# Further expert passes joined to the main pass: their gate and up matmuls, their row fetches and their scatters in a two-layer MoE kernel

## The chip, the cores and the metric

The kernel runs on one core of a Trainium2 chip. The metric is the device time of one execution in microseconds, as the median over several runs. The profile is one execution, recorded by the hardware profiler.

## The reference, cut to what matters

One inference step of a small diffusion backbone: 128 prompt tokens and 256 latent tokens, width 1024, two layers. Layer 0 mixes tokens by differential attention, layer 1 by a Fourier transform. Behind each mixer stands a mixture of experts: a router picks one of 4 groups and in it 2 of 8 experts, so that each of the 384 tokens goes to 2 of 32 gated MLPs.

```python
a = jnp.einsum('nd,edf->nef', t, w_g)          # gate, 1024 -> 256
u = jnp.einsum('nd,edf->nef', t, w_u)          # up,   1024 -> 256
act = jax.nn.silu(a) * u * combine[..., None]  # zero except for the 2 experts of a token
y = jnp.einsum('nef,efd->nd', act, w_d)        # down, 256 -> 1024
x = _post_norm(x, g_f * moe, ln_gain[i, 1], ln_bias[i, 1])
```

## The kernel before

The kernel computes an expert only for its own tokens, in float32. Experts are handled in 16 pairs per layer (`PAIRS`); one **pass** of a pair takes up to 64 tokens (`CAP`) for each of its two experts, which makes 128 rows. Where an expert of the pair has more than 64 tokens, the pair needs **further passes**, up to 5. VectorE counts the tokens (`route`), and packs the number of further passes of each pair, three bits each, into two words (`mem.words`, one for pairs 0 to 7 and one for 8 to 15). Every engine loads these words into a register and loops over the pairs with the loops and branches of `passes` (line 307; POOL and SP have their own loops). `b` is the parity of the pair; most buffers come in two, by parity.

A main pass of pair n, by engine:

- **POOL** (GpSimd) fetches the rows of pair n + 2 from `h_scratch` in HBM into `G[b]` with an indirect gather (`gather`, DMA issue on line 563, behind a copy of the indices on line 559), and writes the pair's results to `y_scratch` with an indirect scatter from `O[b]` (`scatter`, line 576, index copy line 570). A counter `o_free` tells ScalarE and VectorE when `O[b]` may be written.
- **PE** multiplies gate and up (`gate_up`, line 916) into bank b, turns the rows of pair n + 1 (`gt`, line 903), turns the activations (`act_transposes`, line 924) and multiplies down (`down`, line 938) into banks 5 and 6. In the profile's names all on-chip buffers of this stage are `arena`.
- **ScalarE** takes the SiLU of the gate (line 1215), evicts half of the turned rows (line 1210) and half of the result (`o_evict`, line 1220). **VectorE** multiplies by up (`up_times`, line 1662), evicts the other halves (lines 1657 and 1672) and the turned activations (line 1666).
- **SP** loads weights. The ring has four slots, one per expert, two pairs in all. Gate and up of pair n + 2 are issued when pair n, further passes included, has used its own (`u_ps` and `gate_up_through`), down when all its downs are done (`d_ps` and `down_through`, which VectorE raises behind the further pass's `o_evict`). SP waits for these in program order.

A further pass stood behind the whole main pass, as the body of `passes`. On POOL its rows were fetched into `G[2]` in the same pair's turn, and the queue waited for the landing of the main scatter before the further pass could write `O[b]`, and for the landing of its own scatter before going on:

```python
pool.wait_ge(S["gt_ps"], n1)
with pool.If(times > 0):
    gather(extra, l, PAIRS + n, pool.snap(further[pool]), 2)
gather(S, l, n + 2, n + 2, b)
pool.wait_ge(S["scattered"], n16)
scatter(S, l, n, n, b)
with pool.If(times > 0):
    pool.wait_ge(S["scattered"], n32)
    scatter(extra, l, (r + 1) * PAIRS + n, k, b)
    pool.wait_ge(extra["scattered"], k16)
```

## Time and profile before

| | before |
|---|---|
| median of 3 runs | 1063.76 us (1063.31 to 1065.43) |
| the profiled execution | 1065.38 us, span 1063.6 us |
| PE busy | 835.2 us (79%) |
| VectorE, ScalarE, POOL busy | 329.9, 166.0, 158.7 us |
| DMA moved | 318.11 MB, mean 299 GB/s |
| chain that ended last | PE 50%, DMA 35% |

The span runs from the first to the last instruction. Busy time is the time in which an engine executed something; the chain of waits follows the last instruction back through what released each step. All times in the rows below are microseconds from the start of the span.

### The profile page before, as it was taken

Reading aid. Unit: us, or ns where it says so; the run is one execution under the profiler, and the core shown is the slowest. Engines: PE = TensorE matmul, PEld = TensorE weight load, DVE = VectorE, ACT = ScalarE, POOL = GpSimd, SP = SyncE. Lnnn points to the kernel's source line nnn. Section 1 sums busy time; section 2 is a strip of 40 time slices with the busy share of each in tenths; the row PEclk is TensorE's granted clock in tenths of the full one; section 3 lists DMA queues with packets and bytes.
Section 4 is the critical chain, followed back from the end, with each engine's and each line's share of the span. In section 5 each row is a group of like instructions: output and inputs, shape, how many; then the busy total and the mean of one; then the engine's idle time right before and its main releaser. Section 6 shows DMA issues by size and latency. Waiting matters only on the chain.

```text
span 1063.6 us, 13809 instructions
## 1 busy us (share of the span) xinstructions
PE 835.2 (79%) x4921; PEld 442.9 (42%) x4922; DVE 329.9 (31%) x803; ACT 166.0 (16%) x354; POOL 158.7 (15%) x245
## 2 busy tenths in 40 slices
PE   3899999969987888988778855997589877787740
PEld 3556565635466333323323334664533322332310
DVE  2113555544754111111111128247411110111117
ACT  0122222233010111111111112110111111101110
POOL 1032030311111120211101101101111111101010
PEclk9999999989985999989989987999589998999985
DMA  9992653292686496999999889564659999999831
GB/s 336 367 350 91 220 176 130 80 367 82 235 328 248 165 417 260 420 421 420 419 412 407 347 309 375 204 252 178 227 217 421 420 420 419 419 417 413 368 127 79
DMA packets 90242, 318.11 MB, mean 299 GB/s; under 512 B 13150, under 2 KB 26174, under 8 KB 65624
## 3 DMA queue, kind: packets, MB, share of 16 engines
q1 hardware_dynamic: 70016, 274.60, 65.3%
q0 software_dynamic: 13376, 22.16, 6.0%
q10 hardware_dynamic: 6808, 20.79, 5.1%
q8 instruction: 27, 0.44, 0.2%
q14 instruction: 15, 0.12, 0.0%
HBM read 315.82 MB, written 26.80 MB: 322 GB/s over the span
## 4 chain that ended last, share of the span: by engine, by line
PE 50%; DMA 35%; DVE 6%; issue 4%; SPq 2%; ACT 2%; POOL 1%; ACTq 0%; DVEq 0%; POOLq 0%
DMA ring<-in_w_expert_up 24%; PE psum L916 15%; PE psum L799 8%; DMA ring<-in_w_ada 6%; PE psum L745 6%; PE psum L938 4%; PE psum L694 4%; PE psum L771 3%; DMA arena<-h_scratch,gidx 2%; DMA y_scratch<-arena,sidx 2%; PE psum L903 1%; DMA arena<-y_scratch 1%; SPq L366 1%; PE psum L1091 1%; PE psum L850 1%
## 5 line engine op out<-in xcount | busy, mean ns | idle before, releaser
L916 PE MATMUL psum<-ring,arena 128*64 128x512 f32 x1088 | 260.0, 633 | 60.6 <-DMA ring<-in_w_expert_up 56.6
L916 PEld LDWEIGHTS psum<-ring,arena 128*64 128x64 f32 x1088 | 93.4, 146 | 223.2 <-issue 221.1
L938 PE MATMUL psum<-ring,arena 128*64 128x512 f32 x544 | 125.9, 604 | 30.9 <-DVE arena L1666 29.6
L1662 DVE TENSOR_TENSOR arena<-arena,psum 128x256 f32<-128x256 f32 x34 | 14.3, 421 | 309.6 <-ACT arena L1215 309.6
L799 PE MATMUL psum<-ring,hT 128*128 128x384 f32 x288 | 98.2, 495 | 0.0
L938 PEld LDWEIGHTS psum<-ring,arena 128*64 128x64 f32 x544 | 40.2, 138 | 93.2 <-issue 77.8
L694 PE MATMUL psum<-ring,silu 128*32 128x128 f32 x1536 | 55.8, 305 | 27.4 <-DMA ring<-in_w_ada 26.9
L576 POOL DMA_INDIRECT y_scratch<-arena,sidx x34 | 34.4, 1012 | 250.9 <-DVE arena L1672 250.9
L745 PE MATMUL psum<-ring,hT 128*128 128x512 f32 x160 | 70.2, 595 | 1.1 <-ACT hT L1288 0.7
L799 PEld LDWEIGHTS psum<-ring,hT 128*128 128x128 f32 x288 | 54.5, 194 | 35.0 <-issue 1.5
L1672 DVE COPY arena<-psum 128x512 f32<-128x512 f32 x34 | 23.5, 692 | 134.4 <-PE psum L938 134.4
L694 PEld LDWEIGHTS psum<-ring,silu 128*32 128x32 f32 x1536 | 47.6, 123 | 38.1 <-DMA ring<-in_w_ada 19.1
L1215 ACT ACTIVATE arena<-psum 128x256 f32<-128x256 f32 x34 | 13.0, 383 | 273.6 <-PE psum L916 273.6
L903 PEld LDWEIGHTS psum<-k_rows_sb,arena 128*128 128x128 f32 x288 | 35.5, 195 | 33.6 <-issue 26.0
L903 PE MATMUL psum<-k_rows_sb,arena 128*128 128x128 f32 x288 | 42.6, 292 | 5.3 <-DMA arena<-h_scratch,gidx 5.3
L745 PEld LDWEIGHTS psum<-ring,hT 128*128 128x128 f32 x160 | 30.1, 191 | 38.1 <-issue 36.3
L563 POOL DMA_INDIRECT arena<-h_scratch,gidx x38 | 39.7, 1044 | 30.8 <-POOL gidx L559 29.2
L1220 ACT COPY arena<-psum 128x512 f32<-128x512 f32 x34 | 19.9, 585 | 151.3 <-PE psum L938 151.3
L504 POOL TENSOR_TENSOR rstd<-rs_v,power 128x1 f32<-128x1 f32 (+2 forms) x19 | 11.3, 593 | 173.6 <-DVE rs_v L1347 173.6
L771 PE MATMUL psum<-ring,hT 128*128 128x384 f32 x96 | 33.3, 508 | 3.7 <-ACT hT L1150 2.3
L1196 ACT ACTIVATE arena<-psum,nb 128x384 f32<-128x384 f32 (+1 forms) x48 | 24.0, 505 | 49.7 <-DVE nb L1437 49.7
L828 PE MATMUL psum<-arena 64*128 64x384 f32 (+1 forms) x96 | 19.3, 476 | 14.7 <-ACT arena L1196 9.7
(177 smaller groups left out, 796.6 us busy)
## 6 DMA issues: line engine op xcount, KB each, us to landing
ring<-in_w_expert_gate SPq DMA_DIRECT2D x64, 1024.0 KB, 14.1
ring<-in_w_expert_up SPq DMA_DIRECT2D x64, 1024.0 KB, 21.4
ring<-in_w_expert_down SPq DMA_DIRECT2D x64, 1024.0 KB, 19.3
ring<-in_w_ada SPq DMA_DIRECT2D x24, 2048.0 KB, 14.0
ring<-in_w_qkv SPq DMA_DIRECT2D x9, 1024.0 KB, 11.5
arena<-m_scratch POOLq DMA_DIRECT2D x12, 512.0 KB, 7.4
h_scratch<-h ACTq DMA_DIRECT2D x6, 1024.0 KB, 10.3
arena<-y_scratch ACTq DMA_DIRECT2D x6, 1024.0 KB, 7.7
```

Source lines behind the costliest of these rows:

```text
L563: pool.indirect_dma_start(mem.G[b], None, h_dram[l], bass.IndirectOffsetOnAxis(ap=mem.gidx[:, b:b + 1].bitcast(U32), axis=0), bounds_check ...
L576: pool.indirect_dma_start(y_dram[l], bass.IndirectOffsetOnAxis(ap=mem.sidx[:, b:b + 1].bitcast(U32), axis=0), mem.O[b], None, bounds_check ...
L694: last = pe.matmul(out[32 * j:32 * j + 32, :], mem.silu[:, k, :], w[:, k, P * j:P * j + P], start=(k == 0), stop=(k == KC - 1))
L745: last = pe.matmul(bank[banks[half]], mem.hT[:, k, P * t:P * t + P], w[:, k, :], start=(k == 0), stop=(k == KC - 1))
L771: last = pe.matmul(bank[FIRST_BANKS[g]][:, 0:384], mem.hT[:, k, P * t:P * t + P], w[:, k, 384 * half:384 * half + 384], start=(k == 0), st ...
L799: last = pe.matmul(bank[i % 2][:, 0:384], mem.hT[:, k, P * t:P * t + P], w[:, k, 384 * half:384 * half + 384], start=(k == 0), stop=(k == ...
L903: last = pe.transpose(bank[2 + c // 4][:, P * (c % 4):P * (c % 4) + P], mem.G[b][:, c::KC], ident)
L916: last = pe.matmul(bank[b][64 * e:64 * e + 64, :].rearrange("p (g n) -> p g n", g=2), mem.GT[b][:, c, 64 * e:64 * e + 64], w, start=(c == ...
L938: last = pe.matmul(bank[5 + half][64 * e:64 * e + 64, :], mem.actT[b][:, f, 64 * e:64 * e + 64], w[:, f, 512 * half:512 * half + 512], sta ...
L1196: nc.scalar.activation(mem.p[g % 2][j][:, 0:w], bank[5 + j][:, 0:w], ACT.Exp, bias=mem.nb[:, g % 2, j:j + 1], scale=SCALE, accum_out=mem.s ...
L1220: nc.scalar.copy(mem.O[b][:, 0:512], bank[5]).then_inc(S["o_act"], 1)
L1672: V.tensor_copy(mem.O[b][:, 512:D], bank[6]).then_inc(S["o_dve"], 1)
```

## The change

The numbers of further passes are packed into four words: the two as before, and two shifted by one pair, so that a place in them tells of the pair that follows.

On PE, ScalarE and VectorE `passes` now has four parts: `begin` (gate and up of the main pass), then either `alone` (the rest of a main pass without further ones) or `joined`: the further rows are turned, the main activations are turned, gate and up of the first further pass are multiplied, and only then come the main pass's down and the turning of the next pair's rows. `more` finishes a further pass, and starts it too where it is the second or later.

On POOL the rows of a pair's first further pass are fetched in the turn of the pair before, and those of pair 0 ahead of the loop. The scatter of a further pass has a third index column, and its landing is awaited in the next pair's turn (`past`), ahead of the signal `o_free`. The wait for the main scatter stands between that scatter and the further one, as before.

```diff
-        self.words_f = sb("words_f", [P, 2])
-        self.words = sb("words", [P, 2], I32)
+        self.words_f = sb("words_f", [P, 4])
+        self.words = sb("words", [P, 4], I32)
...
-        self.sidx = sb("sidx", [P, 2], I32)
+        self.sidx = sb("sidx", [P, 3], I32)
...
+        self.octals = small(2, PAIRS)
...
-        def passes(eng, l, S, first, body):
...
+        def passes(eng, l, S, begin, alone, joined, more):
...
-                        first(n, b, half * (PAIRS // 4) + it)
                         times = eng.snap((word >> (it * 6 + 3 * b)) & 7, min_val=0, max_val=PASSES - 1)
+                        begin(n, b, half * (PAIRS // 4) + it)
                         with eng.If(times > 0):
+                            joined(n, b, half * (PAIRS // 4) + it, eng.snap(further[eng]))
                             with eng.Fori(0, times) as r:
-                                body(n, b, r + 1, eng.snap(further[eng]))
+                                more(n, b, r, eng.snap(further[eng]))
                                 eng.reg_add(further[eng], further[eng], 1)
+                        with eng.Else():
+                            alone(n, b, half * (PAIRS // 4) + it)
...
+                if l == 0:
+                    pool.dma_start(mem.landing[2:3, :], A["k_rows"][0:1, 0:P]).then_inc(extra["scattered"], 16)
 
                 pool.wait_ge(words_done, l + 1)
+                begin = pool.value_load(mem.words[0:1, 0:1], min_val=0, max_val=(1 << 24) - 1)
+                with pool.If(pool.snap(begin & 7) > 0):
+                    gather(extra, l, PAIRS, pool.snap(further[pool]), 2)
                 with pool.Fori(0, 2) as half:
                     word = pool.value_load(mem.words[0:1, bass.ds(half, 1)], min_val=0, max_val=(1 << 24) - 1)
+                    coming = pool.value_load(mem.words[0:1, bass.ds(half + 2, 1)], min_val=0, max_val=(1 << 24) - 1)
                     with pool.Fori(0, PAIRS // 4) as it:
                         for b in range(2):
                             n = half * (PAIRS // 2) + it * 2 + b
                             n1, n16, n32 = value(n + 1), value(16 * n + 16), value(16 * n + 32)
+                            past = value(16 * pool.snap(further[pool]) + 16)
                             pool.wait_ge(S["gt_ps"], n1)
-                            pool.sem_inc(turns, 1)
-                            times = pool.snap((word >> (it * 6 + 3 * b)) & 7, min_val=0, max_val=PASSES - 1)
-                            with pool.If(times > 0):
-                                gather(extra, l, PAIRS + n, pool.snap(further[pool]), 2)
                             gather(S, l, n + 2, n + 2, b)
                             pool.wait_ge(S["scattered"], n16)
+                            pool.wait_ge(extra["scattered"], past)
                             pool.sem_inc(S["o_free"], 1)
-                            scatter(S, l, n, n, b)
+                            times = pool.snap((word >> (it * 6 + 3 * b)) & 7, min_val=0, max_val=PASSES - 1)
+                            following = pool.snap((coming >> (it * 6 + 3 * b)) & 7, min_val=0, max_val=PASSES - 1)
                             with pool.If(times > 0):
-                                pool.wait_ge(S["scattered"], n32)
-                                pool.sem_inc(turns, 1)
+                                scatter(S, l, n, n, b, b)
                                 with pool.Fori(0, times) as r:
                                     k = pool.snap(further[pool])
                                     k16 = pool.snap(16 * k + 16)
                                     with pool.If(r > 0):
                                         gather(extra, l, (r + 1) * PAIRS + n, k, 2)
+                                    pool.wait_ge(S["scattered"], n32)
+                                    pool.wait_ge(extra["scattered"], k16)
                                     pool.sem_inc(extra["o_free"], 1)
-                                    scatter(extra, l, (r + 1) * PAIRS + n, k, b)
-                                    pool.wait_ge(extra["scattered"], k16)
-                                    pool.sem_inc(turns, 1)
+                                    scatter(extra, l, (r + 1) * PAIRS + n, k, b, 2)
                                     pool.reg_add(further[pool], further[pool], 1)
+                                with pool.If(following > 0):
+                                    gather(extra, l, PAIRS + 1 + n, pool.snap(further[pool]), 2)
+                            with pool.Else():
+                                with pool.If(following > 0):
+                                    gather(extra, l, PAIRS + 1 + n, pool.snap(further[pool]), 2)
+                                scatter(S, l, n, n, b, b)
                 pool.wait_ge(S["scattered"], 16 * PAIRS + 16)
+                pool.wait_ge(extra["scattered"], value(16 * pool.snap(further[pool]) + 16))
...
-                def first(n, b, it):
-
+                def begin(n, b, it):
                     slots = [2 * b + e for e in range(2)]
                     gate_up(S, n, b, slots, [(landed[i], 32 * (it + 1 + l * EXPERTS // SLOTS)) for i in slots])
+
+                def own_down(n, b, it):
+                    slots = [2 * b + e for e in range(2)]
+                    down(S, n, b, slots, [(down_landed[i], 16 * (it + 1 + l * EXPERTS // SLOTS)) for i in slots])
+
+                def alone(n, b, it):
                     gt(S, n + 1, 16 * it + (16, 32)[b], 1 - b)
                     act_transposes(S, n, b)
-                    down(S, n, b, slots, [(down_landed[i], 16 * (it + 1 + l * EXPERTS // SLOTS)) for i in slots])
-
-                def body(n, b, r, k):
+                    own_down(n, b, it)
+
+                def joined(n, b, it, k):
+                    gt(extra, k, 16 * k + 16, 2)
+                    act_transposes(S, n, b)
+                    gate_up(extra, k, b, [2 * b + e for e in range(2)], [])
+                    own_down(n, b, it)
+                    pe.wait_ge(extra["gt_act"], k + 1)
+                    pe.wait_ge(extra["gt_dve"], k + 1)
+                    gt(S, n + 1, 16 * it + (16, 32)[b], 1 - b)
+
+                def more(n, b, r, k):
                     slots = [2 * b + e for e in range(2)]
-                    pe.wait_ge(S["gt_act"], n + 2)
-                    pe.wait_ge(S["gt_dve"], n + 2)
-                    gt(extra, k, 16 * k + 16, 2)
-                    gate_up(extra, k, b, slots, [])
+                    with pe.If(r > 0):
+                        pe.wait_ge(S["gt_act"], n + 2)
+                        pe.wait_ge(S["gt_dve"], n + 2)
+                        gt(extra, k, 16 * k + 16, 2)
+                        gate_up(extra, k, b, slots, [])
                     act_transposes(extra, k, b)
                     pe.wait_ge(S["o_act"], n + 2)
                     pe.wait_ge(S["o_dve"], n + 2)
                     down(extra, k, b, slots, [])
...
-                link(V.tensor_tensor(mem.further, mem.further, mem.const("octal"), ALU.mult))
+                link(V.tensor_tensor(mem.octals[:, 0, :], mem.further, mem.const("octal"), ALU.mult))
+                link(V.tensor_tensor(mem.octals[:, 1, 0:PAIRS - 1], mem.further[:, 1:], mem.const("octal")[:, 0:PAIRS - 1],
+                                     ALU.mult))
+                link(V.memset(mem.octals[:, 1, PAIRS - 1:], 0.0))
                 dve.wait_ge(table_ps, 2 * l + 2)
                 table_evict(slice(PAIRS, PASSES * PAIRS), bank[1][:, 0:(PASSES - 1) * PAIRS])
-                link(V.tensor_reduce(mem.words_f[:, :], mem.further.rearrange("p (h n) -> p h n", h=2), AX, ALU.add))
+                link(V.tensor_reduce(mem.words_f[:, :], mem.octals.rearrange("p w (h n) -> p (w h) n", h=2), AX, ALU.add))
...
-                def first(n, b, it):
-
+                def begin(n, b, it):
                     up_times(S, n, b)
+
+                def alone(n, b, it):
                     gt_evict(S, n + 1, 1 - b)
                     at_evict(S, n, b)
                     o_evict(S, n, b)
 
-                def body(n, b, r, k):
+                def joined(n, b, it, k):
                     gt_evict(extra, k, b)
+                    at_evict(S, n, b)
                     up_times(extra, k, b)
                     dve.sem_inc(gate_up_through, 1)
+                    o_evict(S, n, b)
+                    gt_evict(S, n + 1, 1 - b)
+
+                def more(n, b, r, k):
+                    with dve.If(r > 0):
+                        gt_evict(extra, k, b)
+                        up_times(extra, k, b)
+                        dve.sem_inc(gate_up_through, 1)
                     at_evict(extra, k, b)
                     o_evict(extra, k, b)
                     dve.sem_inc(down_through, 1)
```

ScalarE's parts are cut and ordered like VectorE's; the semaphores of the unused fetch counters are gone.

PE, expert loop of layer 0, pair 0 (L916 gate and up, L903 rows turned, L924 activations turned, L938 down; `main0` and `extra` are the semaphores of main and further passes; rows with a count alone are left out). Before:

```order
L916 MATMUL psum<-ring,arena 64x512 x15
...
L903 MATMUL psum<-k_rows_sb,arena 128x128 [waits gathered1_main0]
...
L924 MATMUL psum<-k_rows_sb,arena 128x128 [waits act_main0]
...
L938 MATMUL psum<-ring,arena 64x512 [waits o_act_main0,o_dve_main0,down_landed1,down_landed0]
...
L319 COMPARE_AND_BRANCH
...
L901 ISA [waits gt_dve_main0,gt_act_main0]
L903 MATMUL psum<-k_rows_sb,arena 128x128 [waits gathered2_extra]
...
L916 MATMUL psum<-ring,arena 64x512 [waits gt_dve_extra,gt_act_extra]
...
L924 MATMUL psum<-k_rows_sb,arena 128x128 [waits act_extra]
...
L938 MATMUL psum<-ring,arena 64x512 [waits o_act_extra,at_sb_extra,o_dve_extra,o_dve_main0,o_act_main0]
```

With the change (L931 gate and up, L918 rows turned, L939 activations turned, L953 down):

```order
L931 MATMUL psum<-ring,arena 64x512 x15
...
L320 COMPARE_AND_BRANCH
...
L918 MATMUL psum<-k_rows_sb,arena 128x128 [waits gathered2_extra]
...
L939 MATMUL psum<-k_rows_sb,arena 128x128 [waits act_main0]
...
L931 MATMUL psum<-ring,arena 64x512 [waits gt_dve_extra,gt_act_extra]
...
L953 MATMUL psum<-ring,arena 64x512 [waits o_act_main0,o_dve_main0,down_landed1,down_landed0]
...
L916 ISA [waits gt_dve_extra,gt_act_extra]
L918 MATMUL psum<-k_rows_sb,arena 128x128 [waits gathered1_main0]
...
L985 COMPARE_AND_BRANCH
...
L939 MATMUL psum<-k_rows_sb,arena 128x128 [waits act_extra]
...
L953 MATMUL psum<-ring,arena 64x512 [waits o_act_extra,at_sb_extra,o_dve_extra,o_dve_main0,o_act_main0]
```

The further gate and up stand ahead of the main down, and their rows are asked for directly behind the main gate and up.

POOL, expert loop of layer 0, even pairs. Before (L563 gather, L576 scatter):

```order
L649 COMPARE_AND_BRANCH
...
L563 DMA arena<-h_scratch,gidx 128x1024 [waits gidx_extra]
...
L563 DMA arena<-h_scratch,gidx 128x1024 [waits gidx_main0]
...
L570 ISA [waits scattered_main0]
...
L576 DMA y_scratch<-arena,sidx 768x1024 [waits o_dve_main0,sidx_main0,o_act_main0]
...
L658 UNCONDITIONAL_BRANCH [waits scattered_main0]
...
L576 DMA y_scratch<-arena,sidx 768x1024 [waits o_act_extra,o_dve_extra]
```

With the change, the even pair's turn with a further pass (L567 gather, L580 scatter), and then the end of the turn: L676 the fetch for the next pair behind a further pass, L679 the same where the pair had none, with the main scatter behind it:

```order
L567 DMA arena<-h_scratch,gidx 128x1024 [waits gidx_main0]
...
L660 ISA [waits scattered_main0]
L664 REGISTER_ALU [waits scattered_extra]
...
L664 COMPARE_AND_BRANCH
...
L580 DMA y_scratch<-arena,sidx 768x1024 [waits o_dve_main0,sidx_main0,o_act_main0]
...
L672 ISA [waits scattered_main0]
L574 ISA [waits scattered_extra]
...
L580 DMA y_scratch<-arena,sidx 768x1024 [waits o_act_extra,o_dve_extra]
```

```order
L676 COMPARE_AND_BRANCH
...
L567 DMA arena<-h_scratch,gidx 128x1024 [waits gidx_extra]
...
L679 COMPARE_AND_BRANCH
...
L567 DMA arena<-h_scratch,gidx 128x1024 [waits gidx_extra]
...
L580 DMA y_scratch<-arena,sidx 768x1024 [waits o_dve_main0,sidx_main0,o_act_main0]
```

The wait for the further scatter moved from behind it into the next turn, where it stands ahead of the fetch for the following pair.

## Rows read from the trace of the kernel before

**Rows 1.** The page's groups: line engine op, out<-in xcount | busy, mean ns | idle

```profile
L1662 DVE TENSOR_TENSOR arena<-arena,psum 128x256 f32<-128x256 f32 x34 | 14.3, 421 | 309.6 <-ACT arena L1215 309.6
```

**Rows 2.** Chain of waits, whole span: start us, us, what

```profile
437.51 20.84 DMA ring<-in_w_expert_up
...
605.40 7.09 PE psum L916 x32
```

**Rows 3.** Stretch of 5 us: engines busy, then PEclk, DMA share, GB/s

```profile
405.00:410.00 5.00, 5.00 (x26) 1.90 (x22) 0.00 (x0) 0.00 (x0) 0.18 (x1) 1.00 0.10 41
```

**Rows 4.** Timeline of PE, 344 to 411: start us, us, operation [idle before]

```profile
344.42 7.09 PE L916 MATMUL psum<-ring,arena 128*64 128x512 f32 x32 [1.09 <-DVE arena L1657]
...
357.60 1.16 PE L903 MATMUL psum<-k_rows_sb,arena 128*128 128x128 f32 x8
359.64 7.09 PE L916 MATMUL psum<-ring,arena 128*64 128x512 f32 x32 [0.88 <-DVE arena L1657]
...
368.86 3.65 PE L938 MATMUL psum<-ring,arena 128*64 128x512 f32 x16 [0.70 <-issue]
372.32 7.07 PE L916 MATMUL psum<-ring,arena 128*64 128x512 f32 x32
...
393.48 1.16 PE L903 MATMUL psum<-k_rows_sb,arena 128*128 128x128 f32 x8 [1.37 <-DMA arena<-h_scratch,gidx]
...
396.05 5.35 PE L938 MATMUL psum<-ring,arena 128*64 128x512 f32 x16 [1.18 <-DVE arena L1666]
...
403.36 7.09 PE L916 MATMUL psum<-ring,arena 128*64 128x512 f32 x32 [0.87 <-DVE arena L1657]
```

**Rows 5.** Timeline of SP's queue: the releases of the weight slots

```profile
367.47 0.35 SPq L366 DMA_DIRECT2D ring<-in_w_expert_gate  x1
...
372.76 1.18 SPq L372 DMA_DIRECT2D ring<-in_w_expert_down  x2
...
411.20 0.34 SPq L366 DMA_DIRECT2D ring<-in_w_expert_gate  x1
...
416.44 0.89 SPq L372 DMA_DIRECT2D ring<-in_w_expert_down  x2
```

**Rows 6.** Source line L563 in 345.8 to 346: the further rows' gather of pair 0

```profile
L563 POOL DMA_INDIRECT arena<-h_scratch,gidx x1: 1079/1079/1079, 345.9 to 345.9; - x1
...
DMA to landing us min/median/max: 7.4/7.4/7.4
```

**Rows 7.** Timeline of POOL, layer 0: gathers L563, scatters L576, index copies

```profile
343.34 0.52 POOL L635 DMA_DIRECT2D landing<-in_k_rows  x1
...
359.34 1.03 POOL L576 DMA_INDIRECT y_scratch<-arena,sidx  x1 [8.25 <-DVE arena L1672]
363.43 0.18 POOL L570 COPY sidx<-table 128x1 int32 x1 [3.06 <-DMA y_scratch<-arena,sidx]
374.07 0.99 POOL L576 DMA_INDIRECT y_scratch<-arena,sidx  x1 [10.45 <-DVE arena L1672]
383.25 0.18 POOL L559 COPY gidx<-table 128x1 int32 x1 [8.19 <-DMA y_scratch<-arena,sidx]
384.25 1.04 POOL L563 DMA_INDIRECT arena<-h_scratch,gidx  x1 [0.82 <-POOL gidx L559]
...
443.59 1.01 POOL L576 DMA_INDIRECT y_scratch<-arena,sidx  x1 [3.99 <-DVE arena L1672]
...
452.31 0.18 POOL L570 COPY sidx<-table 128x1 int32 x1 [5.64 <-DMA y_scratch<-arena,sidx]
```

**Rows 8.** Timeline of PE, two multiplies behind waits for weights

```profile
458.50 10.02 PE L916 MATMUL psum<-ring,arena 128*64 128x512 f32 x32 [3.80 <-DMA ring<-in_w_expert_up]
...
829.53 8.78 PE L916 MATMUL psum<-ring,arena 128*64 128x512 f32 x32 [2.42 <-DMA ring<-in_w_expert_up]
```

**Rows 9.** DMA queues, 440 to 600: the queues that moved anything: packets, MB, share

```profile
q1 hardware_dynamic: 8750, 63.67, 95.6%
q0 software_dynamic: 2921, 2.82, 5.1%
```

More of the change, by code:

```diff
@@ L154, in __init__ @@
         self.w = sb("w", [P, 2, TILES])
[L155 to L156 removed]
+        self.words_f = sb("words_f", [P, 4])
+        self.words = sb("words", [P, 4], I32)
         self.table = sb("table", [P, 8 * PAIRS], I32)
[L159 removed]
+        self.sidx = sb("sidx", [P, 3], I32)
         self.gidx = sb("gidx", [P, 3], I32)
[L161 removed]
+        self.landing = sb("landing", [3, P])
         K = 256
@@ L566, in gather, with scatter @@
                                         ).then_inc(S[f"gathered{b}"], 16)
-            def scatter(S, l, col, n, b):
-                pool.tensor_copy(mem.sidx[:, b:b + 1], mem.table[:, bass.ds(col, 1)]).then_inc(S["sidx"], 1)
+            def scatter(S, l, col, n, b, at):
+                pool.tensor_copy(mem.sidx[:, at:at + 1], mem.table[:, bass.ds(col, 1)]).then_inc(S["sidx"], 1)
                 n1, n2 = value(n + 1), value(n + 2)
@@ L965, in mlp @@
                 gt(S, 0, 16, 0)
-                passes(pe, l, S, first, body)
+                passes(pe, l, S, begin, alone, joined, more)
                 pe.drain().then_inc(mlp_end, 1)
@@ L1243, in mlp @@
                 act.sem_inc(S["o_act"], 1)
-                def first(n, b, it):
+                def begin(n, b, it):
                     silu(S, n, b)
+                def alone(n, b, it):
                     gt_evict(S, n + 1, 1 - b)
                     o_evict(S, n, b)
-                def body(n, b, r, k):
+                def joined(n, b, it, k):
                     gt_evict(extra, k, b)
                     silu(extra, k, b)
+                    o_evict(S, n, b)
+                    gt_evict(S, n + 1, 1 - b)
+                def more(n, b, r, k):
+                    with act.If(r > 0):
+                        gt_evict(extra, k, b)
+                        silu(extra, k, b)
                     o_evict(extra, k, b)
                 gt_evict(S, 0, 0)
-                passes(act, l, S, first, body)
+                passes(act, l, S, begin, alone, joined, more)
                 act.wait_ge(S["gt_dve"], PAIRS + 1)
@@ L1682, in mlp, with begin, alone @@
                 dve.sem_inc(S["o_dve"], 1)
-                def first(n, b, it):
+                def begin(n, b, it):
                     up_times(S, n, b)
+                def alone(n, b, it):
                     gt_evict(S, n + 1, 1 - b)
@@ L1699, in mlp @@
                 gt_evict(S, 0, 0)
-                passes(dve, l, S, first, body)
+                passes(dve, l, S, begin, alone, joined, more)
             def combine(l, tiles):
```

19 lines of the change are left out of this document (11 added, 8 removed).

## The prediction

> **What bounds the kernel now.** I read the page's groups first. The product of gate and up runs x34 where 32 pairs of experts exist [rows 1]: only two further passes are executed, so the change can act in two places alone. The chain of waits says where time goes: from 437.5 us on it is weights arriving, up to the last gate and up of layer 0 at 605.4 [rows 2]. The transfers by stretch [rows 3] show the engines of the DMA at 0.10 in 405 to 410; in 440 to 600 weights and rows fill them [rows 9]. So layer 0 ends when its weights have come. **From the release at 411.2 on the DMA is never idle, since each load is issued before the one ahead is through; what shifts the end is the moment from which it is never idle again, and how much is then left.**
>
> In PE's timeline [rows 4] the passes are found: pair 0 multiplies at 344.4, its further pass at 359.6 (rows turned at 357.6), pair 1 at 372.3; pair 2 follows, and its further pass multiplies at 403.4. In layer 1 there are none. SP's queue [rows 5] shows the releases: gate and up of pair 0's slots at 367.5 (call it G0), down at 372.8 (D0), then G2 at 411.2 and D2 at 416.4. G is 4 transfers of 1.05 MB; at the 66.5 MB in 160 us of a full DMA [rows 9], 416 GB/s, that is 10.1 us, and D, half of it, 5.0. G2 is through at 411.2 + 10.1 = 421.3 (counted from issue), and D2 starts there, though issued at 416.4. **421.3 is the mark**: whatever the change makes of D2's start moves the end of layer 0, and of the kernel, since the mixer behind it waits for the experts.
>
> **Part 1: the further rows of pair 0.** Their gather was issued at 345.9 and landed 7.4 later, at 353.3, beside the last prologue weights [rows 6]. Before, nobody asked until 357.6. Now PE asks when gate and up end, 344.4 + 7.1 = 351.5. One more small copy of 0.5 us stands ahead of the gather (as that at 343.34 [rows 7]), so I put the landing at 353.8: 2.3 us of PE's gain are a new wait. From turning to multiplying 2.0 (357.60 to 359.64), multiplying 7.1: 362.9. The clock: in 393.48 to 396.05 two idle stretches of 1.4 and 1.2 around the same turning were followed by 5.35 for a down of 3.65 [rows 4], half speed (1.2 instead of 2.4 GHz) for a stretch, 1.7 us lost. The same pattern, idle longer, comes here; but at 344.42, 1.1 idle behind the first turning was followed by full speed. Between 0 and 1.7 I take the middle, 0.9. The further multiply ends at **E0 = 363.8** (before 359.64 + 7.09 = 366.7), and G0 goes out 0.7 later, at 364.5 instead of 367.5. PE gains nothing by pair 1: behind the further multiply now stand own down 3.65, turning and small transposes with their evictions 2.5 (393.48 to 396.05), and the further down 3.65, together 9.8, so that pair 1 begins at E0 + 9.8 = 373.6 against 372.3.
>
> **Part 2: the same O buffer.** The further pass's eviction waits until the main pass's scatter has landed, before and now. Before, that scatter went out at 359.3 into an idle DMA, was done by 363.4 [rows 7], and the further multiply covered it. Now own down starts at E0 and the scatter follows 5.2 later (368.86 to 374.07 [rows 4, 7]), at 369.0, with G0's weights in flight. Beside weights a scatter takes 8.7 to the next step of the queue (443.59 to 452.31 [rows 7]), against 4.1 idle. Nearest is the busy row, since G0 moves until about 375: 377.7. So D0 is issued at 378.0, not 372.8. The Trainium skill (DMA: Bandwidth & Descriptors, Anatomy of one DMA) puts a GpSimd transfer at about 2.0 us plus bytes over 436 GB/s, 3.2 us for 0.5 MB; by that the eviction would never be late, and the sum would be the first rival's below, -3.6 instead of +2.7; the rows beside weights do not agree with it. D0 late costs nothing by itself: pair 2 needs it after 390.
>
> **Part 3: the fetch one pair ahead.** The further scatter goes out 1.3 behind D0 (372.76 to 374.07): 379.3. It is not awaited at once, so the gather for pair 3 is issued without the old delay; that removes the wait of 1.37 at 393.48 and the slow clock behind it [rows 4], 3.1 us of PE, but only once PE is past its new wait. But in pair 1 POOL awaits that scatter **before** it issues the further rows of pair 2: 9.2 (374.07 to 383.25), 1.0 to the gather, 9.2 to landing (384.25 to 393.48) [rows 4, 7]. 379.3 + 19.4 = 398.7. From pair 1's start to the end of pair 2's gate and up PE took 393.48 - 1.37 - 372.32 = 19.8, so it is done at 373.6 + 19.8 = 393.4 and idles 5.3 us. Then 2.0 + 7.1 = 407.8. Behind an idle stretch of 3.80 a multiply took 10.02, behind one of 2.42 8.78, against 7.09 [rows 8]: 2.9 or 1.7 lost. Longer than both, yet part of it falls on the turning: I take 2.0. **E1 = 409.8**, before 403.36 + 7.09 = 410.5. G2 goes out at 410.5: 0.7 us gained of all this.
>
> **Part 4: D2.** Own down from E1, main scatter at 415.0, landed 423.7 (8.7 again), further eviction, D2 at **424.0**. G2's weights are through at 410.5 + 10.1 = 420.6. The DMA stands empty for 3.4 us, which it did not before. Against the mark: 424.0 - 421.3 = **+2.7 us**. Pair 3's multiply starts 9.8 behind E1 and takes 7.1, so G3 follows at 427.0 (0.3 for the release); D2 is through at 429.0, so the DMA stays full from there, and the bytes left are the same.
>
> **Edits I cost at nothing.** The two more VectorE operations for the shifted words: at most the 0.4 us of the gate product each [rows 1], done while PE still turns its first rows and their eviction runs; without that cover 0.8 us, once per layer. The branch now between gate and up and the turning: PE went from one pass to the next over two branches without a gap (368.86 + 3.65 against 372.32 [rows 4]). If that cover is gone it is some tenths in eight pairs, those before the DMA is full. ScalarE's table loads keep their number. Late waits for main scatters: in the DMA-bound pairs PE waits for weights, so POOL's order is not seen.
>
> **Sum.** +2.7 against the profiled execution, 1065.38, makes 1068.1; that execution lies 1.6 above the median of the runs, 1063.76, and against the median the forecast is 1066.5.
>
> **Bounds.** The landings of the transfers that the change moves are in no row as they will be; each stands between its idle and its busy row. Low, with the busy landings kept: no slow clock in pair 0 (-0.9), 0.9 less in pair 2, 1.0 less in the gather: about 0. High: the first clock term 1.7, the second 2.9, 1.3 more in the gather (the two landings read, 7.4 and 9.2, are 1.8 apart): +5.7, 1069.5.
>
> **Rivals.**
> - *Faster.* The scatters beside one G of 10 us land as in an idle DMA, 4.1. For it: G0 and G2 are all that is queued, not a full ring as at 443. Against: they move for the whole of those 8 us. Then scatter 0 is done at 373.1 and the eviction waits for its own down only, E0 + 9.9 = 373.7; further scatter 375.3, turning 394.7, E1 = 394.7 + 9.1 + 1.7 = 405.5, D2 at 415.6 before G2 is through; G3 at 422.7 is then what is late, against 411.2 + 15.1 = 426.3: -3.6, 1060.2. It decides from a scatter under about 5 us.
> - *Even.* Half of it: landings some 1 us shorter each, no slow clock. G2 comes 3 us earlier and D2's hole eats it: -1 to +2, about 1064.5.
> - *Code.* PE's loop grows: one pass is 58 matmuls and 58 loads, the loop held 4 passes, 464, and holds about 730 instructions now. A pair takes 15.1 us by its weights and 12.7 by PE (the 19.8 less one multiply). If every jump over the arm not taken had to fetch code, at the 8.7 us of a small transfer beside weights, each pair would grow by 6.3, and some 22 weight-bound pairs would make it about 1200. It decides from a fetch of 2.4 us. Against it: in 440 to 600 the loop turned over and over, and the list of queues has no instruction transfer [rows 9], so more than the 464 stayed at hand. The Trainium skill (Runtime: NRT & Kernel Launch, Instruction fetch mechanics) warns of just this, a taken branch outside a window of two 16 KB pages, and in the same section gives PE room for 2048 instructions; by its two pages, 512 instructions, this rival would hold, by the 2048 not.
> - *It does not do what it says*: the multiply is not directly behind since its rows are late, in both places. That is in the sum.
>
> **Chances.** A measurement tells about 0.2%, 2.1 us. The forecast's case (+2.1 to +5.7) 0.45, faster 0.15, even 0.34, code 0.04, others 0.02 on both sides. So faster 0.16, same 0.34, slower 0.50. The range 1060.5 to 1070.0 reaches from the faster rival to past the upper bound.
>
> **What would show it.** SP's G0 at 364 to 365, D0 over 10 us behind it; PE idle some 5 us before the turning of pair 2; G2 near 410; D2 13 us behind G2, and DMA share near zero for some 3 us before it. Wrong if D2 goes out within 10 us of G2, if the turning of pair 2 comes before 395, or if instruction transfers appear among the pairs.

## The result, and the profile after

| | before | after |
|---|---|---|
| median of 20 runs each | 1063.28 us (1058.68 to 1065.90) | 1067.59 us (1063.42 to 1070.22) |
| the profiled execution | 1065.38 us, span 1063.6 us | 1068.14 us, span 1066.0 us |
| PE busy | 835.2 us | 834.5 us |

The ratio is 1.0042, with a 95% interval of 1.0029 to 1.0054: the change makes the kernel **slower by 4.3 us** (3.1 to 5.7), more than the 0.2% (2.1 us) that the prediction took a measurement to tell. A second comparison, in a later series, gave 1.0032 (1.0016 to 1.0049), +3.4 us.

In the changed kernel gate and up stand on L931, turned rows on L918, downs on L953, the gather on L567, the scatter on L580, VectorE's eviction of the result on L1714, SP's releases on L370 and L376. The timeline of PE, from the first gate and up on, answers to [rows 4]; columns as there:

```profile
341.18 7.09 PE L931 MATMUL psum<-ring,arena 128*64 128x512 f32 x32 [1.09 <-DVE arena L1699]
349.82 1.16 PE L918 MATMUL psum<-k_rows_sb,arena 128*128 128x128 f32 x8 [1.56 <-DMA arena<-h_scratch,gidx]
...
351.85 7.09 PE L931 MATMUL psum<-ring,arena 128*64 128x512 f32 x32 [0.64 <-DVE arena L1699]
358.74 3.63 PE L953 MATMUL psum<-ring,arena 128*64 128x512 f32 x16
...
364.73 3.65 PE L953 MATMUL psum<-ring,arena 128*64 128x512 f32 x16 [1.03 <-issue]
368.19 7.06 PE L931 MATMUL psum<-ring,arena 128*64 128x512 f32 x32
...
394.75 1.97 PE L918 MATMUL psum<-k_rows_sb,arena 128*128 128x128 f32 x8 [6.20 <-DMA arena<-h_scratch,gidx]
...
397.60 8.99 PE L931 MATMUL psum<-ring,arena 128*64 128x512 f32 x32 [0.45 <-DVE arena L1699]
```

Pair 0's further multiply (351.85) stands directly behind its own gate and up, with an idle stretch of 1.56 for the rows. Pair 2's further rows were awaited for 6.20, and its multiply took 8.99 instead of 7.09.

SP's queue, the releases, as [rows 5]:

```profile
359.68 0.35 SPq L370 DMA_DIRECT2D ring<-in_w_expert_gate  x1
...
374.62 1.18 SPq L376 DMA_DIRECT2D ring<-in_w_expert_down  x2
...
407.34 0.34 SPq L370 DMA_DIRECT2D ring<-in_w_expert_gate  x1
...
420.86 0.89 SPq L376 DMA_DIRECT2D ring<-in_w_expert_down  x2
423.08 0.34 SPq L370 DMA_DIRECT2D ring<-in_w_expert_gate  x1
```

D0 lies 14.9 behind G0 and D2 13.5 behind G2; before, they lay 5.3 and 5.2 behind [rows 5].

The chain of waits of the kernel before had at this place one scatter, that of pair 0's further pass, and the gather for pair 3:

```profile
374.07 8.34 DMA y_scratch<-arena,sidx
...
384.25 9.18 DMA arena<-h_scratch,gidx
```

With the change it reads:

```profile
364.05 10.13 DMA y_scratch<-arena,sidx
...
374.40 0.70 DVE arena L1714
...
375.91 8.10 DMA y_scratch<-arena,sidx
...
386.22 8.48 DMA arena<-h_scratch,gidx
...
394.75 1.99 PE psum L918 x8
...
397.60 8.99 PE psum L931 x32
...
605.04 7.09 PE psum L931 x32
```

The main scatter (10.13), the further eviction, the further scatter (8.10) and the gather of pair 2's further rows (8.48) follow one another in POOL's queue, and PE's further multiply of pair 2 stands behind all of them.

The stretches of 5 us, columns as in [rows 3]:

```profile
395.00:400.00 5.00, 4.55 (x16) 2.59 (x17) 1.02 (x2) 0.58 (x1) 0.18 (x1) 0.50 0.84 345
...
415.00:420.00 5.00, 5.00 (x26) 2.05 (x24) 0.00 (x0) 0.00 (x0) 0.00 (x0) 1.00 0.89 365
420.00:425.00 5.00, 4.33 (x24) 2.15 (x20) 2.08 (x4) 1.55 (x3) 2.18 (x4) 1.00 0.61 241
425.00:430.00 5.00, 4.60 (x22) 1.95 (x24) 0.74 (x2) 0.89 (x2) 0.23 (x1) 1.00 1.02 418
```

In 395 to 400 PE's granted clock is 0.50, the lower level. A full stretch reads 1.02 here, so in 415 to 425 the DMA lacks 0.13 and 0.41 of a share, 2.7 us together: the hole between G2's weights and D2.

The stage of experts in layer 0, from the start of the first gate and up to the start of the last, went from 605.40 - 344.42 = 261.0 us to 605.04 - 341.18 = 263.9 us, **+2.9**, where the forecast had +2.7. In the rest of the two spans the part up to the first multiply took 3.2 less, the mixer between the layers 2.3 more, layer 1 0.4 more. The mixer's 2.3 is scatter: in second traces of the two kernels it took 169.0 before and 167.5 with the change. The 3.2 came again (343.9 against 341.1), but the kernel before with one more buffer (experiment 2) started at 340.6 too, so no run shows that this part belongs to the change.

### The profile page after: what moved, and what is told of

It is laid out like the page before. It is cut to its first block, busy times and chain, and to the rows that moved or that the text cites. A ratio compares the mean times of both kernels' runs of the same rounds, so it can differ in the third digit from the quotient of the medians.

```text
span 1066.0 us, 13990 instructions
## 1 busy us (share of the span) xinstructions
PE 834.5 (78%) x4921; PEld 447.8 (42%) x4922; DVE 330.1 (31%) x807; ACT 165.8 (16%) x354; POOL 159.3 (15%) x246
## 4 chain that ended last, share of the span: by engine, by line
PE 46%; DMA 38%; DVE 6%; issue 4%; SPq 2%; POOL 2%; ACT 2%; POOLq 0%; ACTq 0%; DVEq 0%
DMA ring<-in_w_expert_up 24%; PE psum L931 14%; PE psum L814 7%; DMA ring<-in_w_ada 7%; PE psum L760 6%; PE psum L709 4%; PE psum L953 4%; DMA y_scratch<-arena,sidx 3%; DMA arena<-h_scratch,gidx 2%; PE psum L786 1%; DMA arena<-y_scratch 1%; SPq L370 1%; PE psum L918 1%; PE psum L1121 1%; PE psum L865 1%
## 5 line engine op out<-in xcount | busy, mean ns | idle before, releaser
L931 PE MATMUL psum<-ring,arena 128*64 128x512 f32 x1088 | 261.3, 635 | 53.9 <-DMA ring<-in_w_expert_up 50.7
L931 PEld LDWEIGHTS psum<-ring,arena 128*64 128x64 f32 x1088 | 95.1, 146 | 216.0 <-issue 214.4
L953 PE MATMUL psum<-ring,arena 128*64 128x512 f32 x544 | 125.7, 603 | 34.7 <-DVE arena L1708 32.6
L953 PEld LDWEIGHTS psum<-ring,arena 128*64 128x64 f32 x544 | 43.3, 138 | 94.6 <-issue 94.6
L1714 DVE COPY arena<-psum 128x512 f32<-128x512 f32 x34 | 23.5, 692 | 146.6 <-PE psum L953 128.2
L580 POOL DMA_INDIRECT y_scratch<-arena,sidx x34 | 34.5, 1015 | 226.9 <-DVE arena L1714 225.2
L814 PEld LDWEIGHTS psum<-ring,hT 128*128 128x128 f32 x288 | 53.6, 191 | 34.1
L918 PE MATMUL psum<-k_rows_sb,arena 128*128 128x128 f32 x288 | 43.6, 296 | 13.0 <-DMA arena<-h_scratch,gidx 11.9
L918 PEld LDWEIGHTS psum<-k_rows_sb,arena 128*128 128x128 f32 x288 | 36.1, 196 | 40.2 <-issue 26.0
L567 POOL DMA_INDIRECT arena<-h_scratch,gidx x38 | 39.6, 1041 | 30.9 <-POOL gidx L563 30.9
L786 PE MATMUL psum<-ring,hT 128*128 128x384 f32 x96 | 33.3, 508 | 3.7 <-ACT hT L1180 2.2
L574 POOL COPY sidx<-table 128x1 int32 x34 | 6.2, 182 | 190.0 <-DMA y_scratch<-arena,sidx 105.6
L1699 DVE COPY arena<-psum 128x512 f32<-128x512 f32 x36 | 24.9, 692 | 25.4 <-PE psum L918 25.4
## 6 DMA issues: line engine op xcount, KB each, us to landing
ring<-in_w_qkv SPq DMA_DIRECT2D x9, 1024.0 KB, 11.2
```

What stands on the lines that cost most here:

```text
L567: pool.indirect_dma_start(mem.G[b], None, h_dram[l], bass.IndirectOffsetOnAxis(ap=mem.gidx[:, b:b + 1].bitcast(U32), axis=0), bounds_check ...
L580: pool.indirect_dma_start(y_dram[l], bass.IndirectOffsetOnAxis(ap=mem.sidx[:, at:at + 1].bitcast(U32), axis=0), mem.O[b], None, bounds_che ...
L786: last = pe.matmul(bank[FIRST_BANKS[g]][:, 0:384], mem.hT[:, k, P * t:P * t + P], w[:, k, 384 * half:384 * half + 384], start=(k == 0), st ...
L814: last = pe.matmul(bank[i % 2][:, 0:384], mem.hT[:, k, P * t:P * t + P], w[:, k, 384 * half:384 * half + 384], start=(k == 0), stop=(k == ...
L918: last = pe.transpose(bank[2 + c // 4][:, P * (c % 4):P * (c % 4) + P], mem.G[b][:, c::KC], ident)
L931: last = pe.matmul(bank[b][64 * e:64 * e + 64, :].rearrange("p (g n) -> p g n", g=2), mem.GT[b][:, c, 64 * e:64 * e + 64], w, start=(c == ...
```

## The experiments

Two theories went into the runs. **Buffer**: the joined order lets the main scatter be awaited before the further eviction, since both use one result buffer; that D2 and pair 2's rows are late follows from it. **Outside**: something else that the change brought (its larger loop, its words, its branches, its late waits) costs the time.

### 1. The further pass gets a result buffer of its own

```diff
+        self.O.append(self.h[:, 0, :])
...
-                nc.scalar.copy(mem.O[b][:, 0:512], bank[5])
+                nc.scalar.copy(mem.O[2 if S is extra else b][:, 0:512], bank[5])
...
-                V.tensor_copy(mem.O[b][:, 512:D], bank[6])
+                V.tensor_copy(mem.O[2 if S is extra else b][:, 512:D], bank[6])
...
-                                        mem.O[b], None, bounds
+                                        mem.O[at], None, bounds
...
-                                    pool.wait_ge(S["scattered"], n32)
                                     pool.wait_ge(extra["scattered"], k16)
```

> The change, with a result buffer of its own for the further pass (h's first tile, free during the experts), so that its eviction no longer waits for the main scatter. My theory: D0 about 10 us behind G0 instead of 15, further scatter 6 us earlier, and with it the further rows of pair 2; D2 about 10 us behind G2 instead of 13.5; the hole ahead of D2 gone. 1057, from 1054 to 1060. Rival (the DMA or the fetch alone sets the time, the buffer is only seen in the queue): 1064 to 1068.

Measured: 1058.76 us (1055.95 to 1061.87, 12 runs), ratio to before 0.9964 (0.9948 to 0.9980), -3.8 us, inside the expected range. POOL's timeline of this kernel (L581 is the scatter, L568 the gather), and its PE at pair 2:

```profile
364.06 1.03 POOL L581 DMA_INDIRECT y_scratch<-arena,sidx  x1 [17.09 <-DVE arena L1714]
...
369.95 0.99 POOL L581 DMA_INDIRECT y_scratch<-h,sidx  x1 [4.66 <-DVE h L1714]
...
380.66 1.03 POOL L568 DMA_INDIRECT arena<-h_scratch,gidx  x1 [0.83 <-POOL gidx L564]
```

```profile
388.57 1.16 PE L918 MATMUL psum<-k_rows_sb,arena 128*128 128x128 f32 x8
...
390.60 7.09 PE L931 MATMUL psum<-ring,arena 128*64 128x512 f32 x32 [0.60 <-DVE arena L1699]
```

The further scatter follows the main one by 5.9 instead of 11.9, pair 2's rows are there when PE asks, and its multiply takes the 7.09 of full speed. In SP's queue D2 follows G2 by 8.9, before G2's weights are through:

```profile
398.44 0.34 SPq L371 DMA_DIRECT2D ring<-in_w_expert_gate  x1
...
407.36 0.89 SPq L377 DMA_DIRECT2D ring<-in_w_expert_down  x2
```

With this one wait removed, +4 becomes -4: what the joined order lost, it lost by the shared buffer.

### 2. The same buffer in the kernel before

The edit of experiment 1, in the kernel before (which needs a third index column for it).

> The kernel before, with the same result buffer of its own for the further pass and nothing else. Its main scatter was landed 9 us before the further eviction, so my theory says the buffer does nothing there: within 2 us of before (1061 to 1065); the gain of the buffer is only to give back what the joined order lost. Rival (the buffer is worth its 8 us anywhere): 1056 or less.

Measured: 1062.67 us (1060.25 to 1065.78, 12 runs), ratio 1.0001 (0.9985 to 1.0018). In the old order the buffer is worth nothing that shows (1.6 us less to 1.9 us more): the further multiply covers the main scatter. So experiment 1 does not gain by the buffer alone but by the buffer in the joined order.

### 3. Pair 2's further rows fetched ahead of the two scatter waits

```diff
+                            with pool.If(times == 0):
+                                with pool.If(following > 0):
+                                    gather(extra, l, PAIRS + 1 + n, pool.snap(further[pool]), 2)
                             pool.wait_ge(S["scattered"], n16)
                             pool.wait_ge(extra["scattered"], past)
...
                             with pool.Else():
-                                with pool.If(following > 0):
-                                    gather(extra, l, PAIRS + 1 + n, pool.snap(further[pool]), 2)
                                 scatter(S, l, n, n, b, b)
```

> The change, with the following pair's further rows fetched ahead of the two waits for scatters where the pair itself has no further pass. My theory: the rows of pair 2 land some 6 us earlier, PE no longer idles 6 us before turning them, the slow clock behind that goes, G2 and D2 come 8 us earlier than with the change, but D2 stays 13.5 us behind G2: 1059, from 1056 to 1062. Rival (only the eviction matters): no more than 2 us below the change.

Measured: 1063.68 us (1058.07 to 1072.07, 12 runs), ratio 1.0011 (0.9988 to 1.0034): by the ratios 2 to 3 us less than the change (1.0042 and 1.0032), where 8 were expected. The expected range, up to 1062, was missed, and the interval reaches from a small gain to about the loss of the change. POOL and PE of this kernel:

```profile
377.45 1.04 POOL L567 DMA_INDIRECT arena<-h_scratch,gidx  x1 [0.82 <-POOL gidx L563]
...
379.53 1.03 POOL L567 DMA_INDIRECT arena<-h_scratch,gidx  x1 [0.84 <-POOL gidx L563]
```

```profile
390.46 1.97 PE L919 MATMUL psum<-k_rows_sb,arena 128*128 128x128 f32 x8 [2.53 <-DMA arena<-h_scratch,gidx]
...
393.30 9.01 PE L932 MATMUL psum<-ring,arena 128*64 128x512 f32 x32 [0.45 <-DVE arena L1700]
```

From the first multiply the gather went out 4.8 earlier than in the change (40.3 against 45.0), but 2 us behind another gather it took 10.9 to land instead of 8.5, so the turning came only 2.4 earlier. An idle stretch of 2.53 cost as much clock here as one of 6.20 in the change: 1.97 and 9.01 against 1.97 and 8.99. D2 stayed 13.6 behind G2.

### 4 and 5. No further passes at all, in the old and in the new code

```diff
-put("octal", np.tile(8.0 ** (np.arange(PAIRS) % 8), (P, 1)))
+put("octal", np.zeros((P, PAIRS)))
```

and 15 rows of the result, which the further passes would write, are filled by small copies from an input. These two kernels leave out the tokens beyond 64 per expert, so they are not the reference's computation any more; they serve for time alone.

> The kernel before with the table that packs the counts set to zero, so that no further pass runs: the rows beyond 64 per expert are left out (15 rows get a copy of an input row instead). Weights for pair 2 are then released at about 352 instead of 367 and never stop, D2's start moves from 421.3 to about 395: some 26 us less than before, near 1037. It is the partner of the run with the change.

> The change with the same table of zeros and the same 15 rows: its branches, longer loops and shifted words run, its further passes do not. My theory (the whole cost lies in the two further passes) says: same as its partner within 2 us. The rival says that something outside them costs time too, since behind the experts of layer 0 the profiled runs of the change and of both its variants took 461 us where the profiled run before took 458: then it is slower than its partner by 1.5 to 3 us, with the time lost between the experts of layer 0 and those of layer 1.

Measured: the old code 1047.01 us (1043.27 to 1048.16, 5 runs), ratio 0.9839 (0.9814 to 0.9866); the new code 1046.06 us (1044.55 to 1050.14, 5 runs), ratio 0.9845 (0.9821 to 0.9869). The two are the same as far as five runs each can tell: the ratios differ by 0.0006, each with an interval of 0.0025 either way, so four words, more branches and a larger loop do not cost 4 us, but 1.5 us would not have shown. Against the theory that the cost lies outside the further passes stands experiment 1 as well, which has all of this code and gains 3.8 us.

The saving, 16 us, is less than the 26 expected, and the traces tell why. The stage of experts did shorten, from 261.0 and 259.0 to 235.8 in the old code and from 263.9 and 263.1 to 237.3 in the new, by 23 to 27. But the 15 copies stand in ScalarE's queue ahead of work that PE waits for early in layer 0: before the first matmul behind them PE idled 6.28 where it idled 0.77 in the kernel before, and the first gate and up came 4 to 6 later.

```profile
52.84 9.87 ACTq L1166 DMA_DIRECT2D y_scratch<-in_x_sample  x15
...
73.31 0.88 PE L816 MATMUL psum<-k_rows_sb,arena 128*128 128x128 f32 x3 [6.28 <-POOLq L536]
```

### 6 and 7. POOL's part alone, and the joined order alone

POOL as changed, with the old order on PE, ScalarE and VectorE:

```diff
                         begin(n, b, half * (PAIRS // 4) + it)
+                        alone(n, b, half * (PAIRS // 4) + it)
                         with eng.If(times > 0):
-                            joined(n, b, half * (PAIRS // 4) + it, eng.snap(further[eng]))
...
-                        with eng.Else():
-                            alone(n, b, half * (PAIRS // 4) + it)
...
-                    with pe.If(r > 0):
-                        pe.wait_ge(S["gt_act"], n + 2)
+                    pe.wait_ge(S["gt_act"], n + 2)
```

ScalarE's and VectorE's `more` lose their branch in the same way.

> POOL of the change (rows fetched one pair ahead, scatters awaited late), order of before on PE, ScalarE and VectorE (the further pass behind the whole main pass). My theory: the main scatter is again covered by the further multiply, pair 3's rows come early, so PE's wait of 1.4 before pair 2's end and the slow clock behind it go; G2 at about 408 instead of 411.2 and D2 right behind it: 1060 (1058 to 1062), better than before. Rival (late waits and early fetch are what costs): 1065 or more.

Measured: 1060.10 us (1058.11 to 1065.48, 12 runs), ratio 0.9982 (0.9961 to 1.0002), -1.9 us; the interval just reaches no change. PE turned pair 2's further rows without a wait.

The joined order with POOL's loop of the kernel before:

> Order of the change on PE, ScalarE and VectorE, POOL of before. My theory: the eviction behind the main scatter stays as late as in the change, and POOL awaits the further scatter before it fetches anything; pair 2's further rows are fetched behind pair 1's scatter, some 4 us later than in the change: 1071 (1069 to 1074). Rival (the joined order by itself is a gain, POOL's part the loss): 1063 or less.

Measured: 1073.31 us (1070.47 to 1074.39, 6 runs), ratio 1.0084 (1.0062 to 1.0107), +8.9 us. PE at pair 2, and a stretch of 5 us:

```profile
402.10 1.97 PE L907 MATMUL psum<-k_rows_sb,arena 128*128 128x128 f32 x8 [12.98 <-DMA arena<-h_scratch,gidx]
...
404.95 8.96 PE L920 MATMUL psum<-ring,arena 128*64 128x512 f32 x32 [0.45 <-DVE arena L1688]
```

```profile
405.00:410.00 5.00, 5.00 (x16) 1.73 (x18) 0.13 (x1) 0.00 (x0) 0.00 (x0) 0.62 0.00 0
```

The rows come 12.98 late and the DMA has nothing to do. So the order on PE, ScalarE and VectorE is a loss of 9, of which POOL's part gives some 5 back.

### 8. Both repairs

The edits of experiments 1 and 3 together.

> The change with both remedies: a result buffer of its own for the further pass, and the following pair's further rows fetched ahead of the waits. With the own buffer alone PE already turned pair 2's further rows without a wait, so my theory gives nothing on top of it: within 2 us of that run (1058.8), 1056 to 1061. Rival (the fetch behind the scatter still cost something that the slow clock hid): 1055 or less.

Measured: 1057.52 us (1053.36 to 1058.73, 7 runs), ratio 0.9948 (0.9927 to 0.9968), **-5.5 us: faster than both kernels of the comparison**. Its stage is as long as that of experiment 1 (below): with the buffer, the fetch has nothing left to give. That the median is 1.2 lower than there lies within the intervals.

### 9 and 10. Both kernels once more

> The change once more, on this chip beside the others: 1067 (1065 to 1069), by both theories. It tells what two runs of one kernel differ by, and gives the joined order a value in the same series as the buffer.

> The kernel before, one more profile, to see what of the profiled differences outside the experts of layer 0 is spread: my theory puts its stretch from the experts of layer 0 to those of layer 1 near 169 us, as in the changed kernels, and not at the 167.0 of the first profile. Rival: 167 again.

Measured: the change 1065.61 us (1062.84 to 1069.27, 12 runs), ratio 1.0032; the kernel before in one run 1063.15 us, beside a median of 1062.23 of 24 runs. The stretch between the layers took 169.0 in this trace, as expected, and not the 167.0 of the first.

### The ten traces with further passes under one rule

The prediction held that the end of the stage hangs on the moment from which the DMA is never idle again: the issue of D2, or G2 plus 10.1 where D2 is out by then. Both times are counted here from the first multiply of the same trace:

| kernel | mark | last multiply | difference |
|---|---|---|---|
| before | 76.9 | 261.0 | 184.1 |
| before, again | 75.1 | 259.0 | 183.9 |
| before with own buffer | 74.9 | 258.7 | 183.8 |
| POOL's part alone | 75.3 | 259.3 | 184.0 |
| fetch ahead | 77.4 | 261.5 | 184.1 |
| the change | 79.7 | 263.9 | 184.2 |
| the change, again | 78.9 | 263.1 | 184.2 |
| joined order alone | 87.0 | 271.2 | 184.2 |
| own buffer | 67.4 | 252.4 | 185.0 |
| both repairs | 67.5 | 252.5 | 185.0 |

In eight traces, with marks 12 us apart, the difference stays within 0.5, in the old loop and the new. The two at 185.0 have the mark so early that G3 is the later: it is issued at 414.19 in experiment 1, 0.6 behind the end of D2's transfers (398.44 + 15.15). That accounts for 0.6 of their 0.9; over all ten traces, with marks 20 us apart, the rule holds within 1.2. What is outside the stage scatters: the first multiply lies at 339.3 to 344.4, the mixer between the layers (last multiply to first of layer 1) takes 167.0 to 170.9, the rest 289.6 to 292.0. So one profiled span tells little of 3 us. The stage by its own start is better, but it scatters too: before's two traces differ by 2.0 in it. What holds to some tenths is that the end of the stage follows the mark.

## Why the prediction was right

Forecast 1066.5 in a range of 1060.5 to 1070.0, slower the likeliest; measured 1067.59, slower. Its steps, with every time counted from the first multiply (344.42 before, 341.18 after):

| step | forecast | measured |
|---|---|---|
| pair 0's further rows turned | 9.4 | 8.6 |
| end of the further multiply, E0 | 19.4 | 17.8 |
| G0 | 20.1 | 18.5 |
| main scatter issued | 24.6 | 22.9 |
| further eviction may begin | 33.3 | 33.2 |
| D0 | 33.6 | 33.4 |
| gather of pair 2's further rows | 45.1 | 45.0 |
| these rows turned | 54.3 | 53.6 |
| end of their multiply, E1 | 65.4 | 65.4 |
| G2 | 66.1 | 66.2 |
| D2 | 79.6 | 79.7 |
| G3 | 82.6 | 81.9 |
| last multiply of layer 0 | 263.7 | 263.9 |

The signs that the prediction named came, with one caveat. D0 lay over 10 us behind G0, PE idled 6.20, D2 lay 13.5 behind G2. The DMA share fell for about 4 us, from 419 to 423, but only in one of them as low as 0.14; it was not near zero for 3 us. The absolute times did not hold, since the whole stage began 3.2 earlier: G0 went out at 359.7 and not at 364 to 365. By the letter one sign of being wrong came too, the turning of pair 2 before 395: it stood at 394.75. Counted from the first multiply it is 53.6, and the bound is 50.6, so the sign was set in times from the start of the span, which do not carry from one trace to another.

- **Part 1, pair 0.** The landing took 7.8 from the gather (342.02 to 349.82), the new wait was 1.56 instead of 2.3, and the slow clock, put at 0.9, did not come in this trace. E0 was 1.6 earlier than forecast, by two mis-sized terms: the gather went out 0.8 behind the first multiply and not 2.0, and the clock term was put at 0.9 where nothing was lost.
- **Part 2, the O buffer.** The mechanism was right, its size too small: 10.13 for the scatter beside G0's weights instead of 8.7, and 10.35 up to the eviction. This error cancelled that of part 1 to 0.1, so D0 came out right by luck as much as by reason. The Trainium skill's formula for a transfer (DMA: Bandwidth & Descriptors, Anatomy of one DMA), which gives an estimate of 3.2 us for these bytes, is further off than the busy row was: the measurement decides against it here, beside filled queues.
- **Part 3, the fetch.** Right to some tenths, again by two errors that offset: the gather landed in 8.5 instead of 9.2, and the slow clock cost 2.7 (0.81 on the turning, 1.90 on the multiply) instead of 2.0. The idle stretch was 6.20 instead of 5.3, since PE came to it 1.6 earlier and the rows 0.7. The second error is luck of the trace: in the second trace of the change the clock cost 1.3, behind an idle stretch of 6.46 (last section).
- **Part 4, D2.** 13.5 behind G2, as forecast, and +2.8 against the mark of before. Experiment 1 shows that this comes from the buffer, and the table that the end of the stage follows this mark in every trace.
- **Edits at nothing.** Experiments 4 and 5 bear it out to their 4 us, and the code rival, which asked for over 100 us, falls: between 440 and 600 the list of queues of the changed kernel has, as before [rows 9], no instruction transfer (queue, kind: packets, MB, share of the 16 engines):

```profile
q1 hardware_dynamic: 8734, 63.57, 95.5%
q0 software_dynamic: 3041, 2.88, 5.2%
```

  Between 350 and 440 instruction transfers do appear among the pairs, in both kernels: 4 packets before, 6 with the change. No step of the chain of waits stands behind one.

- **Rivals.** *Faster* asked for a scatter under 5 us beside the weights; the shortest that the changed kernel shows in pairs 0 to 2 is the 8.1 of its chain. *Even* asked for landings 1 us shorter each; the gather of pair 2's further rows came near it (0.7 shorter), the main scatter went the other way (1.4 longer).

**The size.** The forecast was +2.7, the stage gave +2.9 (a second pair of traces 263.1 - 259.0 = +4.1), the medians +4.3 and +3.4. The forecast lies just below the first interval (3.1 to 5.7) and inside the second (1.7 to 5.2). Part of the gap is the trace that it started from: before's own mark lay at 76.9 there and at 75.1 in the other trace, while the change's two lie 0.8 apart. Most of the 1.8 is the clock: the down of pair 2 that took 5.35 [rows 4] took 3.65 in the other trace.

```profile
395.12 3.65 PE L938 MATMUL psum<-ring,arena 128*64 128x512 f32 x16 [1.18 <-DVE arena L1666]
```

By the means of two traces each, the change's mark is 3.3 later and its stage 3.5 longer, beside medians of +4.3 and +3.4. So the forecast of +2.7 was somewhat small, and rested on a trace in which before lost 1.7 to the clock.

**What stays open.** Experiment 1 shortened the stage by 7.6 against the mean of before's two, but by the ratio the time fell by 3.8 only. The spans of the profiled executions did fall by 7.4 (1055.1 against 1063.6 and 1061.4). So the gap lies mostly in which executions were profiled: that of experiment 1 was 1.8 below its median, before's two were 2.1 and 0.9 above theirs. What the slower executions of experiment 1 do otherwise, no trace shows. Nor is it known what the 3 us are by which the change's first multiply came earlier.

## What to carry to other kernels

When work is reordered so that a result is written earlier, ask what last read the same buffer, and whether the work that used to stand between covered that transfer: here a scatter of 4 us behind 7 us of matmul became one of 10 us with nothing in front of it, and a buffer of its own for the further pass turned a loss of 4 us into a gain of 4, in the joined order only. In a kernel bound by weights find the moment from which the DMA is never idle again and forecast that: the end of the stage followed it to 0.5 us in eight traces and to 1.2 in all ten. Compare such stages from their own first instruction and in more than one trace, since single spans scatter by as much as the change is worth, and the stage of one kernel differed by 2.0 between two traces.

## What the runs showed of the hardware

- **A landing depends on what is in flight.** Up to the next step of POOL's queue a scatter took 4.1 in an idle DMA [rows 7] and 10.5, 10.7 and 11.2 beside the four transfers of G0 (the change, experiments 3 and 7). A gather 2 us behind another took 10.9 (experiment 3), where one 4.8 later with none just ahead took 8.5 (the change), so issuing earlier bought half of the time it was earlier by. Whether the gather ahead or the weights then in flight made the 2.4, no run separates.
- **The clock.** At pair 2 the granted clock fell to the lower level (1.2 GHz) for a further multiply after an idle stretch of 2.53 as after one of 6.20 or 12.98, and the multiply took 9.01, 8.99 and 8.96 instead of 7.09. The loss does not go by the length of the idle stretch alone: in the second trace of the change it was 7.58 behind 6.46 of idle, the second line below. The first multiply of the stage took 7.09 in some traces and 8.7 in others behind the same idle of 1.09, and that in one and the same kernel: 7.09 in the first trace of the change, 8.72 in its second, the first line below. So these 1.7 us come in some executions and not in others.

```profile
341.11 8.72 PE L931 MATMUL psum<-ring,arena 128*64 128x512 f32 x32 [1.09 <-DVE arena L1699]
...
398.03 7.58 PE L931 MATMUL psum<-ring,arena 128*64 128x512 f32 x32 [0.45 <-DVE arena L1699]
```
